# A four-stage decoder trunk on one core: the last stage's loads in order of need, two weight pieces split on GpSimd, reordered queries and summed means

## The reference: what is computed

```python
x = layer_norm(DEEPNORM_ALPHA * x + mix, ln_g[i, 0], ln_b[i, 0])
ff = swiglu(...) if i % 2 == 0 else moe_swiglu(...)
x = layer_norm(DEEPNORM_ALPHA * x + ff, ln_g[i, 1], ln_b[i, 1])
x = x + (p[i] @ ple_w_proj[i]) * jax.nn.sigmoid(x @ ple_w_gate[i])
```

## Time and profile before

| | us |
|---|---|
| median of 3 runs | 1371.88 (1371.03 to 1373.02) |
| the profiled execution, its own time | 1374.07 |
| its span, from first to last instruction | 1372.4 |
| TensorE busy | 1290.8 (94%) |
| VectorE busy | 654.7 (48%) |
| ScalarE busy | 546.3 (40%) |
| GpSimd busy | 46.4 (3%) |

### The profile page before, as it was taken

One profiled execution on the slowest core, in us unless ns is written; L12 is line 12 of the kernel. 1 busy time (PEld: TensorE's weight loads), 2 busy tenths in 40 slices (PEclk: granted clock), 3 DMA queues, 4 the chain that ended last, 5 costly groups with the idle time before them and its releaser, 6 DMA issues.

```text
span 1372.4 us, 17426 instructions
## 1 busy us (share of the span) xinstructions
PE 1290.8 (94%) x6493; PEld 1087.2 (79%) x6494; DVE 654.7 (48%) x863; ACT 546.3 (40%) x744; POOL 46.4 (3%) x64
## 2 busy tenths in 40 slices
PE   7999999899999999998989999998789999999568
PEld 6889998588888878886876899985778798878457
DVE  5334444633333322325542554455655654567664
ACT  3225442632233222225332333335644644467722
POOL 0000000000000000000000000000100211011000
PEclk9999999999999999999999999999899999989879
DMA  7331123133333333212325642123875885589831
GB/s 186 93 107 47 47 62 92 31 104 96 101 97 92 113 106 105 84 53 81 87 77 79 80 72 55 54 78 99 279 262 157 293 273 178 178 288 311 317 137 62
DMA packets 197959, 175.45 MB, mean 128 GB/s; under 512 B 7248, under 2 KB 178320, under 8 KB 197904
## 3 DMA queue, kind: packets, MB, share of 16 engines
q1 hardware_dynamic: 194016, 160.53, 40.7%
q0 software_dynamic: 3312, 12.06, 2.3%
q10 hardware_dynamic: 576, 2.10, 0.4%
HBM read 164.71 MB, written 9.96 MB: 127 GB/s over the span
## 4 chain that ended last, share of the span: by engine, by line
PE 87%; DMA 4%; DVE 4%; ACT 3%; issue 2%; ACTq 0%; POOLq 0%; POOL 0%; DVEq 0%; SPq 0%
PE bank L694 27%; PE bank L695 26%; PE bank L696 26%; PE bank L791 2%; DVE w_lo L1632 1%; DMA x_back<-x_dram 1%; PE bank L1062 1%; DMA ring<-moe_w_down 1%; DMA y_dram<-y_tok,store_i 1%; DMA xg<-x_dram,gather_i 1%; DMA xg<-x_dram,token_i 1%; PE bank L1015 1%; PE bank L942 1%; PE bank L1110 0%; PE bank L881 0%
## 5 line engine op out<-in xcount | busy, mean ns | idle before, releaser
L1632 DVE TENSOR_TENSOR w_lo<-raw,w_hi 128x1024 fp32r<-128x1024 f32 (+4 forms) x208 | 287.1, 1385 | 210.8 <-ACT w_hi L1216 147.8
L694 PE MATMUL bank<-x_hi,w_hi 128*128 128x512 f32 x672 | 265.8, 396 | 15.3 <-DVE w_lo L1632 7.0
L695 PE MATMUL bank<-x_lo,w_hi 128*128 128x512 f32 x672 | 264.0, 393 | 0.0
L696 PE MATMUL bank<-x_hi,w_lo 128*128 128x512 f32 x672 | 263.6, 392 | 0.0
L1216 ACT CAST w_hi<-raw 128x1024 fp32r<-128x1024 f32 (+2 forms) x141 | 149.7, 1062 | 128.3 <-PE bank L696 128.3
L694 PE MATMUL bank<-w_hi,x_hi 128*128 128x256 f32 (+2 forms) x608 | 191.0, 314 | 8.7 <-DVE w_lo L1632 3.3
L695 PE MATMUL bank<-w_lo,x_hi 128*128 128x256 f32 (+2 forms) x608 | 188.1, 309 | 0.0
L696 PE MATMUL bank<-w_hi,x_lo 128*128 128x256 f32 (+2 forms) x608 | 187.9, 309 | 0.0
L694 PEld LDWEIGHTS bank<-x_hi,w_hi 128*128 128x128 f32 x672 | 127.6, 190 | 47.1 <-DVE w_lo L1632 14.0
L696 PEld LDWEIGHTS bank<-x_hi,w_lo 128*128 128x128 f32 x672 | 127.6, 190 | 27.1
L695 PEld LDWEIGHTS bank<-x_lo,w_hi 128*128 128x128 f32 x672 | 127.8, 190 | 25.7
(11 more groups left out here) (307 smaller groups left out, 1793.1 us busy)
## 6 DMA issues: line engine op xcount, KB each, us to landing
raw<-moe_w_gu SPq DMA_DIRECT2D x32, 768.0 KB, 6.3
raw<-ffn_w_gu SPq DMA_DIRECT2D x44, 512.0 KB, 3.8
raw<-a_w_qkv SPq DMA_DIRECT2D x24, 512.0 KB, 3.7
raw<-moe_w_down SPq DMA_DIRECT2D x16, 768.0 KB, 6.4
raw<-ffn_w_down SPq DMA_DIRECT2D x16, 704.0 KB, 4.3
ring<-moe_w_gu SPq DMA_DIRECT2D x16, 640.0 KB, 7.5
raw<-moe_w_gu SPq DMA_DIRECT2D x16, 640.0 KB, 5.1
raw<-ple_w_gate SPq DMA_DIRECT2D x16, 512.0 KB, 5.8
```

The lines of the kernel that those rows point to most:

```text
L694: pe.matmul(o, s_hi, m_hi, start=start, stop=False, skip_group_check=True)
L695: pe.matmul(o, s_hi, m_lo, start=False, stop=False, skip_group_check=True)
L696: return pe.matmul(o, s_lo, m_hi, start=False, stop=stop, skip_group_check=True)
L1632: return dve.tensor_tensor(dst, a, b, ALU.subtract)
```

## The change

It has five parts. (1) The means: VectorE adds up tiles 0 to 6 in `y_sum` as they arrive, in place of making `x_lo`; ScalarE's cast goes, and TensorE multiplies `y_sum` and tile 7 by the 1/1024 matrix as two plain float32 matmuls. VectorE's loop over phase down is written out for this. (2) At gate0's end, ScalarE casts tiles 0 and 1 of the next `x_hi` before the last sigmoid, and tile 2 behind it; VectorE follows; the wait for the second weight chunk moves to the place where it is first used, in gu, gate0 and q1. In the normalisation ahead of gate0 the split of gate0's second chunk moves later on ScalarE and VectorE. (3) The logits of `w_f` become 24 fp32r matmuls, with `w_f` split on VectorE. (4) The last stage: `g_row` and `b_row` load ahead of the experts, behind a wait for the third mean; `x_back` is four tiles, the first of which ScalarE scales out of `x_rows` ahead of the experts and keeps; behind chunks 0 to 3 of gate1 SP waits for the scatter at once, and then loads tile 0 of `y_one` and `y_two`, chunks 4 and 5, tile 1 of all three, chunks 6 and 7, and the rest. ScalarE and VectorE take chunks 4 to 7 behind tile 0. (5) The low parts of chunks 6 and 7 are made by GpSimd, and TensorE waits for `rest_ready` there. The diff without its unchanged lines, its renamings and its declarations:

```diff
+            sp_eng.wait_ge(turned, KD + 1 + 2 * KP)
+            sp_eng.wait_ge(mean_done, 3)
+            for row, w in ((g_row, ln_g), (b_row, ln_b)):
+                sp_eng.dma_start(row[:, :], w.rearrange("l w d -> (l w) d")[3:4, :].to_broadcast([P, D])).then_inc(rows_loaded, 16)
             def raw_free(e, c):
...
-            for row, w in ((g_row, ln_g), (b_row, ln_b)):
-                sp_eng.dma_start(row[:, :], w.rearrange("l w d -> (l w) d")[3:4, :].to_broadcast([P, D])).then_inc(rows_loaded, 16)
-            sp_eng.wait_ge(lo_ready, low_count(NE - 1, 11))
-            sp_eng.dma_start(x_back[:, :, :], x_dram.rearrange("(t p) d -> p t d", p=P)).then_inc(x_returned, 16)
-            for c in range(RAW, COUNT["gate1"]):
-                load_gate(c)
+                if t:
+                    sp_eng.dma_start(x_back[t][:, :], x_dram[t * P:(t + 1) * P, :]).then_inc(x_returned[t], 16)
+                if t < 2:
+                    load_gate(RAW + 2 * t)
+                    load_gate(RAW + 2 * t + 1)
...
+            for c in (6, 7):
+                n = SIZE["gate1"]
+                pool.wait_ge(hi_ready, BASE["gate1"] + c + 1)
+                pool.tensor_tensor(gate_lo[c][:, 0:n], raw[c % RAW][:, 0:n], gate_hi[c][:, 0:n].bitcast(F32), ALU.subtract
+                                   ).then_inc(rest_ready, 1)
...
-                        if name != "q0":
-                            weights(q, 1)
-                            if name == "q0" and k in (0, LAG):
+                            if k in (0, LAG):
...
-                pe.matmul(bank[4][:, :], mean_r[:, :], x_hi[:, k, :], start=k == 0, stop=False)
-                mm = pe.matmul(bank[4][:, :], mean_r[:, :], x_lo[:, k, :], start=False, stop=k == KD - 1)
-                if k == KD - 1:
-                    mm.then_inc(mean_done, 1)
+            def mean(n):
+                name = ("o0", "down", "o1")[n]
+                pe.wait_ge(drained, DRAINED[name] + COUNT[name] - COUNT[name] // KD)
+                pe.wait_ge(gathered, (KD - 2) * (n + 1))
+                pe.matmul(bank[4][:, :], mean_f[:, :], y_sum[:, :], start=True, stop=False)
+                pe.wait_ge(summed, KD * (n + 1))
+                pe.matmul(bank[4][:, :], mean_f[:, :], x_exact[:, KD - 1, :], start=False, stop=True).then_inc(mean_done, 1)
             def variance(n):
...
-            pe.wait_ge(embedded, KD)
+            pe.wait_ge(f_split, 2)
-                mm = pe.matmul(bank[4][0:H, :], w_f[:, k, :], x_exact[:, k, :], start=k == 0, stop=k == KD - 1)
+                mm = mm3(bank[4][0:H, :], w_f_hi[:, k, :], w_f_lo[:, k, :], x_hi[:, k, :], x_lo[:, k, :], k == 0, k == KD - 1)
...
-                        if t == 0:
+                        if t == 0 and 4 * h + c < 6:
+                        elif t == 0:
+                            pe.wait_ge(rest_ready, 4 * h + c - 5)
...
+                    if last:
+                        embedded_hi(0)
+                        embedded_hi(1)
                 if layer == 0:
+                    embedded_hi(2)
-                    for k in range(KD):
-                        act.wait_ge(embedded, k + 1)
-                        act.copy(x_hi[:, k, :], x_exact[:, k, :]).then_inc(affine, 1)
+                    for k in range(3, KD):
+                        embedded_hi(k)
...
+            act.activation(x_back[0][:, :], x_rows[:, 0, :], ACT.Copy, scale=ALPHA).then_inc(x_scaled, 1)
+            act.wait_ge(x_scaled, 1)
...
             def sigmoid(t):
-                    act.activation(x_back[:, t, h * 512:(h + 1) * 512], bank[t % 2 * 2 + h][:, :], ACT.Sigmoid
+                    act.activation(x_back[t][:, h * 512:(h + 1) * 512], bank[t % 2 * 2 + h][:, :], ACT.Sigmoid
-            act.wait_ge(x_returned, 16)
-            for t in range(TT):
-                op = act.activation(x_back[:, t, :], x_back[:, t, :], ACT.Copy, scale=ALPHA)
-            op.then_inc(x_scaled, 1)
+            def scale_x(t):
+                act.wait_ge(x_returned[t], 16)
+                act.activation(x_back[t][:, :], x_back[t][:, :], ACT.Copy, scale=ALPHA).then_inc(x_scaled, 1)
+            gate_high(3)
-            for c in range(DEEP - 1, COUNT["gate1"]):
-                gate_high(c)
+            gate_high(4)
+            gate_high(5)
+            scale_x(1)
+            gate_high(6)
+            gate_high(7)
+            scale_x(2)
+            scale_x(3)
...
-            def sum_low(n, k):
-                dve.wait_ge(y_hi_ready, KD * n + k + 1)
-                return minus(x_lo[:, k, :], x_exact[:, k, :], x_hi[:, k, :].bitcast(F32))
             def add_residual(n, k, psum):
-                return sum_low(n, k)
+                if 0 < k < KD - 1:
+                    dve.wait_ge(summed, KD * n + k + 1)
+                    if k > 1:
+                        dve.wait_ge(gathered, (KD - 2) * n + k - 1)
+                    before = x_exact[:, 0, :] if k == 1 else y_sum[:, :]
+                    dve.tensor_tensor(y_sum[:, :], before, x_exact[:, k, :], ALU.add).then_inc(gathered, 1)
+                return dve.nop()
             def residual(name, n):
                 def step(q, i, j, last):
...
-                        second_early("gate0")
+                    if n == 1 and k == 6:
+                        second_early("gate0")
...
+                    if last:
+                        embedded_lo(0)
+                        embedded_lo(1)
...
                 if layer == 0:
+                    embedded_lo(2)
-                    for k in range(KD):
-                        dve.wait_ge(affine, KD + k + 1)
-                        minus(x_lo[:, k, :], x_exact[:, k, :], x_hi[:, k, :].bitcast(F32)).then_inc(x_ready, 1)
+                    for k in range(3, KD):
+                        embedded_lo(k)
-            dve.tensor_copy(mean_r[:, :], mean_f[:, :])
...
+            dve.wait_ge(small_loaded, 48)
+            dve.tensor_copy(w_f_hi[:, :, :], w_f[:, :, :]).then_inc(f_split, 1)
+            dve.wait_ge(f_split, 1)
+            minus(w_f_lo[:, :, :], w_f[:, :, :], w_f_hi[:, :, :].bitcast(F32)).then_inc(f_split, 1)
...
             def combine(t):
+                dve.wait_ge(x_scaled, t + 1)
-                                         in1=x_back[:, t, :], op0=ALU.mult, op1=ALU.add).then_inc(first_added, 1)
+                                         in1=x_back[t][:, :], op0=ALU.mult, op1=ALU.add).then_inc(first_added, 1)
...
+            gate_low(4)
+            gate_low(5)
```

57 lines of the change are left out of this document (27 added, 30 removed).

## The result

The changed kernel took 1364.74 us (median of 6 executions, 1360.76 to 1367.70), the kernel before 1371.85 us on the same chip (6, 1369.56 to 1375.81). The ratio is 0.9942, with a 95% interval of 0.9925 to 0.9959: 7.1 us faster, where 16.7 were forecast and 1351 to 1362 was the range. The profiled execution took 1367.70 us, the slowest of its six; its span is 1366.0 us, 6.4 less than before, and all that follows divides these 6.4.

A forecast was written before the change was run, and what follows sets the result against it. The prediction took TensorE's matmuls and its waits to bound the kernel (87% of the chain). Gains of 5.3 + 3.2 + 1.5 + 6.7 = 16.7 us took the median from 1371.88 to 1355.2 us, range 1351 to 1362.

The forecast's parts named there:

- The means: Ends of the residual phases: centring starts 1.7 us sooner in the first, 1.9 in the second, 5.3 us over three.
- `w_f`: Logits of `w_f`: 24 matmuls of 0.227 us take 5.45 us for 7.03, 1.5 us less.
- gate0 to q1: TensorE's wait between gate0 and q1 falls from 4.03 to 2.5 us; gain 3.2 us if the clock stays up.
- the break at the fourth input: In q1, after 9 matmuls, TensorE waits 1.1 us for the weight chunk and the fourth input's low part.
- the other end that the forecast had named: Gate0 to q1 with the clock not staying up: a gain of 1.8 us.
- Before the experts: Scaling of `x_back` tile 0 and two row loads moved ahead of the experts: hidden, cost 0.
- Scatter to transposes: Last stage: scatter lands in 4.0 us, `combine` starts at 1301.6 for 1308.33; gain 6.7 us.
- the rival of the "issue" gap: Last stage: the gap goes, as the program ahead is shorter and DMA engines emptier; 19.0 us gained, 1352.9 us, chance 0.14.
- GpSimd's splits: Last stage, gate1 chunks 6 and 7: GpSimd takes 2.2 to 3 us each, in time, cost 0.
- the first rival: Last stage: VectorE and GpSimd exclude one another, 2.4 us lost; 14.3 us gained, 1357.6 us, chance 0.25.
- The "issue" gap: Last stage, between sixth and seventh transpose: TensorE's 2.95 us loss stays, gain 0, with 2.3 us as the other end.
- the forecast's third rival: Last stage: the issue gap between transposes goes; 19.0 us gained, 1352.9 us, chance 0.14.

The follow-up runs named there:

- after_again: The changed kernel run once more with no edit, against the kernel before: 1360.93 us, ratio 0.9910.
- front_only: The kernel before with all of the change but the last stage's part (summed means, reordered gate0 and q1 start, `w_f` split): 1364.84 us, ratio 0.9943.
- before_pad204: The kernel before with 204 empty instructions at the start of TensorE's program: 1402.49 us, ratio 1.0224.
- no_split_spread: The changed kernel with GpSimd's two splits back on VectorE and 52 empty instructions spread over TensorE's idle places: 1356.56 us, ratio 0.9887.

## Why the prediction was wrong

**Right, in mechanism and size.** The means: 1.8 us in the first and 1.9 in the second, for 1.7 and 1.9. `w_f`: the copy of the logits is 1.45 us further ahead, for 1.5. gate0 to q1: an idle time of 2.63 us for 2.5, the break at the fourth input, and the full clock throughout in six profiles of twelve; in the one profiled first it was the low one, the other end that the forecast had named. The whole is 2.7 us there and 2.9 in after_again, for 3.2. Up to the router 9.4 us (10.5 in after_again, 10.1 in front_only) for 10.0. The row loads and the scaling cost nothing, as costed. Scatter to transposes: 7.8 us less for 6.7; `y_one` was asked for 4.2 us behind the scatter, as forecast, and `combine` began 3.7 us later for 4.8.

**The step that failed** is the one that has no term: the sum goes from the router to the last scatter as if a shorter program for TensorE had no effect but its matmuls. "Before the experts" priced the scaling and the loads at 0, and that held; what came late was TensorE's own instructions. 4.4 us were lost there (9.44 us for 5.07; 2.6 in after_again), shown by making the stall vanish with 52 empty instructions and by making it appear in the kernel before. The forecast had the thought, but only as a gain, in the rival of the "issue" gap ("since the program ahead is shorter"). The Trainium skill has the rule in "Runtime: NRT & Kernel Launch", section on instruction fetch mechanics: instructions come in blocks of 16 KB over the DMA engines, and a taken branch to a place that isn't there waits for a fetch. The trace agrees with the size (37 packets, 0.61 MB on the page) and with the place: the stall stands at the entry into the experts' loop, and ends a steady 3.5 to 3.8 us after the end of a packet. That the fetch is its cause rests on this timing; that the length of the program decides is shown by the edits.

**Two terms mis-sized in the last stage.** GpSimd's splits, taken at 0, cost 1.7 us: the first rival, forecast at 2.4, is what happened, with 2.35 us for an operation as scaled (2.2) and VectorE held. The "issue" gap, kept at 2.95 us, was 4.56; from the transposes of tile 0 to the end 62.8 us, without the gap 58.0, so that it costs 4.8 us (in the version without GpSimd's splits the same: 61.1 and 56.3). The old gap of 2.95 us cost 1.9 to 3.5 (58.5 us in the kernel before, without a gap 56.6 in before_pad204 and 55.1 in front_only), so its growth is 1.3 to 2.9, and 2.6 are left of the 4.3 lost behind the transposes: it fits, but isn't measured apart. In 11 of 14 profiles there was no gap at all, which is the forecast's third rival; its reason, the shorter program, is not borne out, since kernels with the same program on TensorE differ.

**The balance** of the profiled execution: 16.7 forecast, - 0.6 up to the router, - 1.3 in the routing (low clock), - 4.4 at expert 0, - 0.9 in the experts, + 1.1 from scatter to transposes, - 4.3 behind them: 6.3, for 6.4 measured. The 0.6 isn't q1's low clock, which cost 0.2 us against after_again. It is down's start: after a wait of 3.19 us in both kernels the clock stayed low for longer than in the kernel before, and 1.1 us of the lead were lost; half of that was won elsewhere. The 7 us from down's first matmul, before and after (the third number from the end is the granted clock):

```profile
500.70:507.70 7.00, 7.00 (x24) 5.63 (x25) 1.62 (x1) 0.13 (x1) 0.00 (x0) 0.76 0.35 103
```

```profile
498.45:505.45 7.00, 7.00 (x19) 5.54 (x20) 1.62 (x1) 0.14 (x1) 0.00 (x0) 0.58 0.36 103
```

**Chance.** The median of the first set lies 2.7 us outside the range, less than the 3.8 us between the two sets of the same kernel, so on which side of 1362 it fell was chance; that both gain far less than 16.7 is not. Executions of the changed kernel spread from 1354.59 to 1367.70 us together with their granted clock, and the sum holds a term for the clock at q1 alone.

**Open.** What decides whether TensorE's packet in the last stage is fetched during the last expert or only after it: of the 14 profiles shown here beside that of the kernel before, 3 have the gap of 4.6 us and 11 have none, and kernels with the same program on TensorE differ in it. What lets the clock fall in the routing in 9 of these profiles and stay up in the others: not the row loads. Whether the stalls are as long in the executions that weren't profiled wasn't measured; the median without the stall at expert 0 and without the splits (no_split_spread, 1356.56) is 4.7 us below the 1361.3 of the twelve executions, for the 6.1 us that the two terms sum to.
